# Compressed attention in two batches, its products in another order, and gate products spread over all head units

## The reference

```python
kc = compress(k_cmp, cmp_pos[0], cmp_w1[0], cmp_w2[0])     # 31 compressed keys per group
vc = compress(v_cmp, cmp_pos[1], cmp_w1[1], cmp_w2[1])
s = einsum('btgjd,bngd->btgjn', q, kc) * scale
p_cmp = where(c_valid, softmax(where(c_valid, s, NEG_INF)), 0)
o_cmp = einsum('btgjn,bngd->btgjd', p_cmp, vc)
...
qr, ks, kw = rope(q), rope(k_slc), rope(k_win)
o_slc, o_win = softmax attention of qr with ks, v_slc and with kw, v_win
o = g[..., 0:1] * o_cmp + g[..., 1:2] * o_slc + g[..., 2:3] * o_win
...
merged = sigmoid(g_a) * (y_da @ w_proj_da) + sigmoid(g_b) * (y_ns @ w_proj_nsa)
```

## Time and profile before

| | |
|---|---|
| median of 3 runs | 2197.55 us (2194.5 to 2203.15) |
| profiled execution | 2197.66 us, its span 2195.9 us |
| busy | TensorE 2074.9 us (94%), VectorE 1051.0 (48%), ScalarE 822.4 (37%), GpSimd 283.8 (13%) |
| loads and stores | 200.14 MB, mean 91 GB/s |

### The profile page before, as it was taken

The page is one execution under the profiler, slowest core; times in us unless marked ns, Lnnn a source line. Parts: engine busy times, 40 slices in busy tenths (PEclk is TensorE's granted clock), DMA queues, the critical chain, the costliest instruction groups (busy, mean ns, idle before and its releaser), DMA issues.

```text
span 2195.9 us, 25916 instructions
## 1 busy us (share of the span) xinstructions
PE 2074.9 (94%) x10292; PEld 1745.5 (79%) x10292; DVE 1051.0 (48%) x1668; ACT 822.4 (37%) x1526; POOL 283.8 (13%) x271
## 2 busy tenths in 40 slices
PE   7999999999999999999998889788989999999998
PEld 6878888888888888888887778567777888888886
DVE  5437475555344222335546764655655445222333
ACT  5225353334334222334325742255555433222232
POOL 1001000000000000000013431066665000000000
PEclk9997799999999999999998998799999999999999
DMA  5330133333323333332541062111113532333331
GB/s 193 111 91 1 58 112 100 97 96 96 96 68 115 96 96 97 98 99 81 149 129 31 1 215 63 59 43 44 44 44 118 160 92 96 96 96 98 99 100 68
DMA packets 59752, 200.14 MB, mean 91 GB/s; under 512 B 8081, under 2 KB 8113, under 8 KB 59505
## 3 DMA queue, kind: packets, MB, share of 16 engines
q1 hardware_dynamic: 53936, 178.29, 26.4%
q0 software_dynamic: 5696, 20.21, 2.7%
HBM read 181.16 MB, written 8.39 MB: 86 GB/s over the span
## 4 chain that ended last, share of the span: by engine, by line
PE 76%; DVE 8%; ACT 5%; POOL 4%; issue 2%; DMA 2%; DVEq 2%; POOLq 0%; SPq 0%; ACTq 0%
PE ps L649 24%; PE ps L651 23%; PE ps L650 23%; POOL PU L605 4%; DMA raw<-in_w_all 2%; DVE Wl L1658 1%; PE ps L979 1%; PE ps L1064 1%; DVE XN L1698 1%; ACT Pb L1357 1%; DVE HTl L1707 1%; DVEq L2181 1%; ACT XN L1224 1%; DVE AUl L2186 1%; PE ps L824 1%
## 5 line engine op out<-in xcount | busy, mean ns | idle before, releaser
L1658 DVE TENSOR_TENSOR Wl<-raw,Wh 128x1024 fp32r<-128x1024 f32 x307 | 377.9, 1235 | 787.3 <-ACT Wh L1191 786.5
L649 PE MATMUL ps<-HTh,Wh 128*128 128x512 f32 (+1 forms) x1696 | 644.3, 380 | 21.8 <-DVE HTl L1707 10.8
L650 PE MATMUL ps<-HTl,Wh 128*128 128x512 f32 (+1 forms) x1696 | 637.9, 376 | 0.0
L651 PE MATMUL ps<-HTh,Wl 128*128 128x512 f32 (+1 forms) x1696 | 637.9, 376 | 0.0
L1191 ACT CAST Wh<-raw 128x1024 fp32r<-128x1024 f32 x307 | 321.5, 1052 | 820.6 <-DMA raw<-in_w_all 820.5
L649 PEld LDWEIGHTS ps<-HTh,Wh 128*128 128x128 f32 x1696 | 322.6, 190 | 80.0 <-issue 20.8
L651 PEld LDWEIGHTS ps<-HTh,Wl 128*128 128x128 f32 x1696 | 321.6, 190 | 58.2
L650 PEld LDWEIGHTS ps<-HTl,Wh 128*128 128x128 f32 x1696 | 322.4, 190 | 55.7
L649 PE MATMUL ps<-Wh,Yh 128*128 128x512 f32 x528 | 206.1, 390 | 4.3 <-DVE Yl L1834 4.3
L651 PE MATMUL ps<-Wh,Yl 128*128 128x512 f32 x528 | 205.5, 389 | 0.0
L650 PE MATMUL ps<-Wl,Yh 128*128 128x512 f32 x528 | 205.4, 389 | 0.0
(11 more groups left out here) (272 smaller groups left out, 2562.9 us busy)
## 6 DMA issues: line engine op xcount, KB each, us to landing
raw<-in_w_all SPq DMA_DIRECT2D x307, 512.0 KB, 3.6
swp_d<-qkd SPq DMA_DIRECT2D x64, 64.0 KB, 2.8
g_dram<-gst SPq DMA_DIRECT2D x16, 256.0 KB, 4.0
ring<-g_dram POOLq DMA_DIRECT2D x16, 256.0 KB, 3.5
gpre<-in_g_pre POOLq DMA_DIRECT2D x5, 512.0 KB, 5.3
X<-in_x SPq DMA_DIRECT2D x4, 512.0 KB, 5.4
swp_r<-qkr SPq DMA_DIRECT2D x16, 128.0 KB, 3.8
cw1k<-in_cw POOLq DMA_DIRECT2D x1, 2048.0 KB, 10.7
```

What stands on the lines that cost most here:

```text
L649: tensor.matmul(dst, a_hi, b_hi, start=start, stop=False)
L650: tensor.matmul(dst, a_hi, b_lo, start=False, stop=False)
L651: return tensor.matmul(dst, a_lo, b_hi, start=False, stop=stop)
L1658: vector.tensor_tensor(Wl[:, s, :], raw[:, s, :], Wh[:, s, :], ALU.subtract).then_inc(w_lo, 1)
```

## The change

- `cmpa` works on one group of heads at once: two batches of 16 score matmuls (banks 4 and 5), 992 columns for `cmp_shift`, `cmp_exp` and `cmp_weigh` (`CS[g]` has its own place for each group; `CP` is gone), 8 transposes into two banks.
- TensorE's order in `rope_q` is new: `rope_q(1)` ahead of `cmp_hidden(0)`, `cmp_scores(0)` behind `rope_q(3)`, then `cmp_hidden(1)`, and `cmp_turn(0)` behind `rope_q(6)`. The other engines' order follows. `vcz` is made within `rope_q`.
- `ksh` is copied and `ksl` made after `vhl`'s parts; the two key tiles are turned with two splits between them.
- The gate work goes by single depth steps: 16 ahead of the units, then 3 in even and 4 in odd units, all 32 of them. Steps up to the end of a gate product (`cut`) stand ahead of `unit_scores(s + 2)`, the others behind it. In the units ScalarE does `gate_out`.
- `cw1` is laid out so that each partition reads 16 KB in one piece, and GpSimd computes `cA` of kind 0 ahead of the load of `cw1v`.

```diff
-    ("cmpa", 0, [0] * 8, [0, 0, 0, 8, 4, 4, 0, 0]),
+    ("cmpa", 0, [0] * 8, [0, 0, 1, 2, 3, 2, 0, 0]),
...
-        HALVES = [n for n in range(32) if n % 8 != 7]
-        HALF_AT = {s: 4 + n for n, s in enumerate(HALVES)}
+        STEP0 = [16 + 7 * s // 2 for s in range(33)]
...
+        def steps(s):
+            a, b = STEP0[s], STEP0[s + 1]
+            cut = b // 8 * 8
+            return (a, cut, b) if cut > a else (a, a, b)
+        def begun(s):
+            return [n // 8 for n in range(STEP0[s], STEP0[s + 1]) if n % 8 == 0]
...
-                load(cw1k[:], t["cw1"][0].rearrange("(j p) n -> p j n", p=P), in_cw)
+                load(cw1k[:].rearrange("p j n -> p (j n)"), t["cw1"][0], in_cw)
...
-                pl.wait_ge(yd_out, 16 * TT)
-                load(cw1v[:], t["cw1"][1].rearrange("(j p) n -> p j n", p=P), in_cwv)
-                pl.wait_ge(in_pos, 16)
...
+                pl.wait_ge(in_pos, 16)
+                inputs(0)
+                pl.wait_ge(yd_out, 16 * TT)
+                load(cw1v[:].rearrange("p j n -> p (j n)"), t["cw1"][1], in_cwv)
+                inputs(1)
...
                 rope_q(0)
+                rope_q(1)
                 cmp_hidden(0)
-                rope_q(1)
-                cmp_hidden(1)
                 rope_q(2)
                 cmp_keys()
                 rope_q(3)
-                cmp_vals()
-                rope_q(4)
                 pe.wait_ge(free[7], FREED["rope_q"][7] + 2)
                 cmp_scores(0)
+                cmp_hidden(1)
+                rope_q(4)
+                cmp_vals()
                 rope_q(5)
+                rope_q(6)
                 cmp_turn(0)
-                cmp_scores(1)
-                rope_q(6)
-                cmp_turn(1)
-                cmp_scores(2)
                 rope_q(7)
-                cmp_turn(2)
-                cmp_scores(3)
...
                 pe.wait_ge(free[7], FREED["rope_q"][7] + 4)
-                cmp_scores(4)
-                gate_half(0)
...
-                unit_scores(0)
-                cmp_turn(7)
+                cmp_scores(1)
+                unit_scores(0)
+                gate_steps(0, 4)
                 unit_scores(1)
+                gate_steps(4, 8)
+                gate_steps(8, 12)
+                cmp_turn(1)
+                gate_steps(12, 16)
                 for s in range(32):
+                    a, cut, b = steps(s)
                     unit_turn(s)
+                    gate_steps(a, cut)
                     if s < 30:
                         unit_scores(s + 2)
-                    if s in HALF_AT:
-                        gate_half(HALF_AT[s])
+                    gate_steps(cut, b)
                     unit_values(s)
```

ScalarE (first block) and VectorE (the others):

```diff
-                ac.wait_ge(ks_f, 1)
-                scalar.copy(ksh[:]...
...
                 for c in range(8):
                     split(CHUNK0["rope_q"] + c + LEAD)
...
                     query(c)
-                    if c < 2:
-                        hidden(c)
+                    if c == 0:
+                        ac.wait_ge(ks_f, 1)
+                        scalar.copy(ksh[:]...
+                    if c == 1:
+                        hidden(0)
                     if c == 2:
                         cmp_keys()
+                    if c == 3:
+                        cmp_exp(0)
+                        hidden(1)
...
+                    if c == 6:
+                        cmp_high(0)
...
+                cmp_exp(1)
+                unit_exps(0)
                 split(CHUNK0["nsa"] + LEAD)
...
                 split(CHUNK0["nsa"] + 1 + LEAD)
...
                 unit_exps(1)
+                cmp_high(1)
                 for s in range(32):
                     unit_high(s)
+                    a, cut, b = steps(s)
                     if s and s % 2 == 0:
                         head_low(s // 2 - 1)
+                    if a < cut < b:
+                        gate_out(cut // 8 - 1)
                     if s < 30:
                         unit_exps(s + 2)
...
+                    if a < cut == b:
+                        gate_out(cut // 8 - 1)
+                    for c in begun(s):
+                        split(CHUNK0["nsa"] + c + LEAD)
```

```diff
                 for c in range(8):
                     split(CHUNK0["rope_q"] + c + LEAD)
...
                     if c:
                         turn_query(c - 1)
...
+                    if c == 3:
+                        cmp_shift(0)
+                    if c == 4:
+                        cmp_weigh(0)
                         spread_hidden()
...
+                cmp_shift(1)
+                unit_max(0)
+                turn_query(7)
+                unit_gate(0)
+                cmp_weigh(1)
+                gate_out(0)
                 split(CHUNK0["nsa"] + LEAD)
...
+                unit_max(1)
                 split(CHUNK0["nsa"] + 1 + LEAD)
...
+                cmp_low(1)
                 gate_out(1)
```

More of the change, by code:

```diff
@@ L1574, in unit_high, with gate_out @@
                     scalar.copy(AUh[:, 1024:1280], ps[5][:, 0:256]).then_inc(u_hi, 1)
+                def gate_out(c):
+                    chunk_done("nsa", c)
+                    if c >= 2:
+                        ac.wait_ge(g_out[c % 2], 16 * (c // 2))
+                    scalar.copy(gst[c % 2][:], ps[7][:]).then_inc(free[7], 1)
                 def head_low(h):
@@ L2068, in _, with keys_out @@
                 ve.wait_ge(in_rope, 64)
-                for kind in range(2):
+                def keys_out(kind):
                     turned(SWAP0["nsf"] + kind, swp_n)
@@ L2077, in _ @@
                     last.then_inc(roped, 1)
+                keys_out(0)
+                split(CHUNK0["nst"] + LEAD)
+                split(CHUNK0["nst"] + 1 + LEAD)
+                keys_out(1)
                 vector.drain().then_inc(ks_f, 1)
             if on("nst"):
-                for c in range(3):
-                    split(CHUNK0["nst"] + c + LEAD)
-                ve.wait_ge(ks_hi, 1)
-                vector.tensor_tensor(ksl[:].rearrange("p a g n -> p (a g n)"), ksw[:].rearrange("p a g n -> p (a g n)"),
-                                     ksh[:].rearrange("p a g n -> p (a g n)"), ALU.subtract)
+                split(CHUNK0["nst"] + 2 + LEAD)
                 for tt in range(TT):
@@ new lines, in cmp_weigh @@
+                def cmp_weigh(g):
+                    s_ = CS[g][:, :, 0:N_CMP]
+                    by_tile = lambda a: a.rearrange("p (i h) -> p i h", i=TT)
+                    ve.wait_ge(cm_e, g + 1)
+                    vector.tensor_reduce(cst[:, g, 1, :], s_, AX.X, ALU.add)
+                    gate = gates[:, :, 24 * g:24 * g + 24].rearrange("p i (h c) -> p i h c", c=3)[:, :, :, 0]
+                    vector.tensor_tensor(by_tile(cst[:, g, 2, :]), gate,
+                                         cvalid[:].rearrange("p (i a) -> p i a", a=1).broadcast_to((P, TT, 8)), ALU.mult)
+                    vector.drain()
+                    vector.reciprocal(cst[:, g, 1, :], cst[:, g, 1, :])
@@ L2151, in _, with cmp_low @@
+                def cmp_low(g):
+                    for f in range(2):
+                        ve.wait_ge(ca_hi, 2 * g + f + 1)
+                        vector.tensor_tensor(CAl[:, g, f, :], ps[2 + g + f][:], CAh[:, g, f, :], ALU.subtract).then_inc(free[2 + g + f], 1)
                 vector.drain()
@@ L2155, in _ @@
                     split(CHUNK0["rope_q"] + c + LEAD)
-                    if c >= 5:
-                        cmp_shift(c - 5)
-                    if c >= 6:
-                        cmp_low(c - 6)
-                    if c >= 5:
-                        cmp_weigh(c - 5)
                     if c:
                         turn_query(c - 1)
-                    if c == 2:
-                        spread_hidden()
-                cmp_shift(3)
-                cmp_low(2)
-                cmp_weigh(3)
-                turn_query(7)
+                    if c == 1:
+                        ve.wait_ge(ks_hi, 1)
+                        vector.tensor_tensor(ksl[:].rearrange("p a g n -> p (a g n)"), ksw[:].rearrange("p a g n -> p (a g n)"),
+                                             ksh[:].rearrange("p a g n -> p (a g n)"), ALU.subtract)
+                        vector.drain()
+                    if c == 3:
+                        cmp_shift(0)
+                    if c == 4:
+                        cmp_weigh(0)
+                        spread_hidden()
+                    if c == 4:
+                        vector.drain()
+                        vector.memset(vcz[:].bitcast(F32), 0.0)
+                        vector.drain().then_inc(vc_zero, 1)
+                    if c == 6:
+                        ve.wait_ge(vc_hi, 1)
+                        for a in range(4):
+                            q = slice(32 * a, 32 * a + 32)
+                            last = vector.tensor_tensor(vcz[q, :, a, HD:P], ps[1][q, 0:2 * HD].rearrange("p (g d) -> p g d", g=2), vcz[q, :, a, 0:HD],
```

(10 more changed lines are left out.)

193 lines of the change are left out of this document (67 added, 126 removed).

## The result

| | before | after |
|---|---|---|
| median of 7 runs, us | 2197.55 (2191.53 to 2204.59) | 2188.69 (2170.57 to 2190.18) |
| profiled execution, us | 2197.66 (span 2195.9) | 2190.18 (span 2188.4) |
| ratio | 1 | 0.9945 [0.9919, 0.9971] |

The gain is 8.9 us where 39.1 was predicted; 2188.7 lies above the range. Executions of one kernel lie up to 20 us apart here, most of it in the first block's attention (granted clock 0.73 to 0.90 from 160 to 220 us, which the diff doesn't touch), so medians are compared, and traces only with this in mind. I read the page first. Its first rows are span and busy time by engine, then the shares of the chain that ended last, then the costliest group.

What follows compares the result with a forecast made beforehand. TensorE, 76% of the chain that ended last, was taken as the bound, with gains only where it waits or runs at lower clock. First stretch 37.2 + units 4.1 - end 2.2 = 39.1; 2197.66 - 39.1 = 2158.6 us, range 2146 to 2175.

Steps and rivals of the forecast that it cites:

- The rest: Everything outside the first stretch, the units and their end: `cw1` loads are off the path, so no change in time.
- Pure work, 82.8: First stretch, `rope_q(0)` to the first unit: TensorE's work at full clock without gaps, 82.8 us, all kept by the change.
- First gap gone, 9.6 + 6.6: Before `cmp_hidden(0)`: the 9.6 us gap and the 6.6 us of low clock behind it both go.
- The rival by which this gap stays in part: Bank 0 comes late, `cmp_hidden(0)` is slow again: about 10 us lost, 2168.6 us; chance 0.12.
- The wait before `cmp_vals`, 6.0 + 2.4: New wait for `hid_v` on VectorE in the first stretch: TensorE idle 6.0 us, then 2.4 us of low clock.
- The rival without this wait (2150): VectorE gets ahead and the 6.0 + 2.4 us before `cmp_vals` shrink to near nothing: 2150 us; chance 0.10.
- The small waits, 0.85 twice and 3.3: 0.85 us behind each of `rope_q(3)` and `rope_q(7)`; at the start of `nsa` 0.8, 1.75 and 0.75, together 3.3.
- The units, 4.1 gained: The 31 unit periods go from 246.0 to 241.9 us, gaining in units without gate work; bounds 0 to 8.2.
- The ring of 7.67: Unit period: turn, ScalarE's high parts, VectorE's low parts, `ugg`, GpSimd's multiply, next turn; 7.67 us, unchanged.
- The spread does nothing: Rival: late chunks eat what units without gate work cost; the loop stays at 246, 2162.7 us; chance 0.13.
- The end, 2.2 lost: Unit 31 now has four gate steps, delaying the `HTh` copies before `project("pns", 0)`: 2.2 us lost (0.7 to 3).
- The clock rival (2222): Short idle times in every unit make TensorE fall to 1.2 GHz: 64 us more, 2222 us; chance 0.05.

Runs made afterwards that it cites:

- after_base: The changed kernel with the larger `cst` in free room at the end of SBUF, all other tiles at the addresses of before; 2158.77 us.
- gate_hid_first: `gate_first` with VectorE making `hid_v` (`spread_hidden`) ahead of the split that stood before it; 2118.79 us, ratio 0.9627 to before.
- gate_first: `after_base` with `unit_gate(s + 1)` ahead of `unit_low(s)` on VectorE; 2128.85 us, ratio 0.970 to before.
- no_spread: `after_base` with gate steps as before: four in each unit, none in units 7, 15, 23 and 31; 2158.14 us, ratio 0.981 to before.

## Why the prediction was wrong, step by step

**Where it failed.** The step is the sentence "The rest. `cw1` in 16 KB rows changes loads off the path", and the sum behind it, which takes 2197.66 less the three terms: all stages outside the two stretches were held at their old length. The growth of `cst` is a wider tile for VectorE and also a shift of every tile behind it, and the sum has no term for the second. By the account above the untouched stages took 22.9 + 8.5 = 31.4 us more, and with the addresses of before the same change runs at 2158.8. No rival covered it, and the range had no room for a cost in untouched stages. It was in the diff, as the new size of a tile ahead of the slots; nothing in the trace of before shows what a shift costs, so its price could not be had from there, but "matmuls are slower everywhere" could have been a case with a chance.

**Pure work, 82.8.** Too low by 1.5, and made good by luck. `after_base` has the pitch that the prediction reckoned with, and its stretch is 96.8. With 9.2 of idle time and 3.3 of low clock taken off, 84.3 are left: the two score batches took 7.2 where the sum has 6.5, and the 16 gate steps 11.8 where it has 11.2. In after the slower pitch adds another 1.0. The stretch of after still came out within 0.9 of the 96.2, because TensorE's waits were 8.9 there and not 1.7 + 6.0 + 3.3 = 11.0. The agreement of `after_base`'s median with 2158.6 rests on this too.

**First gap gone, 9.6 + 6.6.** Right. TensorE's timeline of after, then VectorE's:

```profile
1338.82 7.25 PE L992 MATMUL ps<-cA,cw1k 128*128 128x62 f32 x64
```

```profile
1335.00 1.67 DVE L2105 TENSOR_TENSOR vhl<-ps,vhl 128x128 fp32r<-128x128 f32 x8 [1.51 <-ACT gates L1526]
```

No idle time, and 7.25 where before had 13.88; the clock is 1.00. VectorE's subtractions began 3.8 us before TensorE came, and the second of them, which gives bank 0, ended 3.3 before (predicted 2.3 to 5 of room). The rival by which this gap stays in part didn't happen.

**The wait before `cmp_vals`, 6.0 + 2.4.** Right: 5.53 + 2.8.

```profile
1380.47 1.97 PE L1009 MATMUL ps<-w2v,hid 128*128 128x64 f32 x8 [5.53 <-DVE hid L2118]
```

```profile
1370.60 2.07 DVE L1672 TENSOR_TENSOR Wl<-raw,Wh 128x1024 fp32r<-128x1024 f32 x1 [5.12 <-ACT Wh L1199]
...
1376.07 1.18 DVE L2151 TENSOR_REDUCE cst<-CS 128x32 f32<-128x992 f32 x1
...
1378.12 1.19 DVE L2160 TENSOR_TENSOR CS<-CS,cst 128x992 f32<-128x992 f32 x1
...
1379.93 0.49 DVE L2118 COPY hid<-hid 128x248 f32<-128x248 f32 x2
```

The releaser is the copy into `hid4` as forecast, the split ahead of it takes the same 2.07, and 992 columns took 1.18 and 1.19 (1.2 worked out from the rows of 248 and 512 columns). The clock behind it is 0.50, that is 1.2 GHz; `cmp_vals` took 1.73 start to start instead of 0.8, and the two products behind it 13.2 instead of some 11.3 at after's own pace. The rival without this wait (2150) didn't happen; `gate_hid_first` shows the edit that it takes.

**The small waits, 0.85 twice and 3.3.** The two behind query copies were 0.69 each. At the start of `nsa` they were 0.51, 1.23 and 0.17, 1.9 in all where 3.3 stood: the terms "0.8", "1.75" and "0.75" were each too large. A lead that VectorE and ScalarE gained while TensorE stood before `cmp_vals` isn't the whole reason: in `gate_hid_first`, without that wait, they still come to 1.9 (0.88 and 1.01), though part of that stretch ran at the low clock. The reason stays open.

**The units, 4.1 gained.** 5.0 measured. The ring of 7.67 is right: it stayed so in most periods, GpSimd's multiply stayed the releaser, and `gate_first` broke it as the reading demands. The late chunks cost less than thought: three periods of 8.05 and single ones of 8.42, 7.75 and 7.72. One unit, though, shows the mechanism at its worst (VectorE, then TensorE, of after):

```profile
1533.97 1.22 DVE L1672 TENSOR_TENSOR Wl<-raw,Wh 128x1024 fp32r<-128x1024 f32 x1 [3.22 <-ACT Wh L1199]
...
1535.11 0.68 DVE L2212 TENSOR_TENSOR AUl<-ps,AUh 128x512 fp32r<-128x512 f32 x1
```

```profile
1532.58 1.31 PE L1076 MATMUL ps<-ident,PU 128*128 128x128 f32 x10 [0.56 <-POOL PU L618]
...
1541.46 1.31 PE L1076 MATMUL ps<-ident,PU 128*128 128x128 f32 x10 [1.64 <-POOL PU L618]
```

The split waited 3.22 us for ScalarE's cast of a late chunk, the low parts stood behind it and began 2.5 us after the turn, and the period is 8.88. The excess over 31 x 7.67 is 3.2 where 4.1 was worked out. But the reason given for the gain promised too much: `no_spread`, in which three units have no gate work, loses only 2.2 in the loop. Of the 3.1 us between before's loop and that of `no_spread`, 1.8 is the first unit (9.40 in before, 7.64 here), which the new order ahead of the units mended, and the rest is that the three periods behind units without gate work came out shorter (8.80, 9.87 and 8.72, in before 9.96, 8.93 and 9.82), as they do between two executions of before. "The spread does nothing" had a loop of 246 as its sign, which is wrong, and a net effect of nothing, which is what the medians show.

**The end, 2.2 lost.** 2.5 lost: the last part of `HTl` came 11.7 us after the last turn (11.5 predicted; before 9.2).

```profile
1676.79 0.69 DVE L2266 TENSOR_TENSOR HTl<-qnr,HTh 128x512 fp32r<-128x512 f32 x1 [0.69 <-ACT HTh L1640]
```

**The clock rival (2222).** It didn't happen. TensorE stood idle 0.55 to 0.92 us in most of the units, as predicted, and the granted clock of the 31 periods is 1.00 (0.96 in before, with its three gaps of some 3.5). By the rule of the Trainium skill, "TensorE: Matmul & The Clock Gate", section "A second HAM failure mode: psum-queue depth-cycling", frequent short idle times would make the clock swing; at this length, once in 7.67 us, the trace doesn't agree.

## What to carry to other kernels

Before a tile changes its size, look at what is allocated behind it: a change can be right in each of its terms and lose them to a shift of the operands, so compare the pitch of the same matmuls in a stage that the diff doesn't touch before any of its waits is explained. Keep the tiles that TensorE reads one after the other at the same place within 256 bytes, if they are like the ones here. And where a period is a ring through several engines, what pays is taking a member out of it (27 us in the loop for two swapped calls), not more work for TensorE to fill the gap (2.2).

## What the runs showed of the hardware

**Placement.** The 512-column matmuls with a weight load each start every 0.2267 us where all operands lie alike within 256 bytes, and every 0.229 to 0.233 where they don't, 1 to 3%; on this kernel 27 to 29 us. It needs neither another engine's work nor a transfer: in after, from 330 to 1000 us, the 578 pairs of starts around which (0.15 us ahead to 0.24 behind) no instruction of VectorE, ScalarE or GpSimd ran are 0.2304 apart, the 1257 around which no DMA packet was under way 0.2305, and the 946 with both 0.2304 (before: 0.2267 in all three). The Trainium skill, "TensorE: Matmul & The Clock Gate", section "Step-by-step: what each phase is for", says that TensorE has two read ports, so that loading the next weights takes no read bandwidth from the running matmul. The pitch here depends on where the one operand lies relative to the other, which that sentence gives no reason for; no run here shows where in the chip the time goes.

**Narrow matmuls and the clock.** The same 64 entries of 62 columns ran at 0.50 for 13.4 us on end in before, behind a gap of 9.60, and at 1.00 throughout in after, entered without a gap. Unbroken work of this kind kept the clock that it found; in before it rose only in the product of 512 columns behind it. Nor do such matmuls always keep the higher one: in `gate_hid_first` the clock fell to 0.50 during the 32 entries of 64 columns of `cmp_scores(1)`, behind 0.69 us of idle, and in `gate_first` the same entries behind the same idle time ran at 1.00.
